# Splitting a weight slab on GpSimd and multiplying half of it over all 512 tokens, at three norms of a two-layer decoder

## The reference, cut to what matters

```
for l in range(2):
    x = layer_norm(ALPHA * x + 0.5 * swiglu(x, ffn1_w_gu[l], ffn1_w_down[l]), ...)
    x = layer_norm(ALPHA * x + hybrid_mixer(x, ...), ...)
    x = layer_norm(ALPHA * x + 0.5 * swiglu(x, ffn2_w_gu[l], ffn2_w_down[l]), ...)

def swiglu(x, w_gu, w_down):          # w_gu: 1024 x 5632, w_down: 2816 x 1024
    g, u = split(x @ w_gu, 2)
    return (silu(g) * u) @ w_down
```

## Time and profile before

| | |
|---|---|
| median of 3 runs | 2403.43 us (2401.1 to 2403.76) |
| the profiled execution: its own time | 2402.06 us |
| the profiled execution: span of the core | 2400.3 us |
| PE busy | 2386.8 us (99% of the span) |
| DVE, ACT busy | 1060.1 us (44%), 759.4 us (32%) |
| POOL busy | 16.0 us (1%) in 16 instructions |
| granted PE clock | 0.999 of full speed, mean of the execution |

### The profile page before, as it was taken

The page is one execution under the profiler, slowest core; times in us unless marked ns, Lnnn a source line. Parts: engine busy times, 40 slices in busy tenths (PEclk is TensorE's granted clock), DMA queues, the critical chain, the costliest instruction groups (busy, mean ns, idle before and its releaser), DMA issues.

```text
span 2400.3 us, 27151 instructions
## 1 busy us (share of the span) xinstructions
PE 2386.8 (99%) x11560; PEld 2005.9 (84%) x11560; DVE 1060.1 (44%) x1590; ACT 759.4 (32%) x1137; POOL 16.0 (1%) x16
## 2 busy tenths in 40 slices
PE   8999999999999999999999999999999999999998
PEld 8888888888888888888888888888888888888887
DVE  4233236554654643322543332465455647333324
ACT  4232223434442332322232221243344433232211
POOL 0000200000000000000000000000000000000000
PEclk9999999999999999999999999999999999999999
DMA  5322433223223333232232332343223323332232
GB/s 167 106 96 97 144 103 124 90 82 95 90 92 123 109 105 103 88 106 104 89 106 89 105 104 89 103 132 94 88 92 97 101 93 132 96 97 97 89 117 75
DMA packets 210536, 246.58 MB, mean 103 GB/s; under 512 B 10576, under 2 KB 172400, under 8 KB 210416
## 3 DMA queue, kind: packets, MB, share of 16 engines
q1 hardware_dynamic: 210416, 244.85, 31.4%
HBM read 238.51 MB, written 6.31 MB: 102 GB/s over the span
## 4 chain that ended last, share of the span: by engine, by line
PE 99%; DVE 1%; DMA 0%; ACT 0%; issue 0%; SPq 0%; DVEq 0%
PE main L1334 22%; PE main L1336 22%; PE main L1335 22%; PE main L1434 5%; PE main L1436 5%; PE main L1435 5%; PE side L1436 4%; PE side L1435 4%; PE side L1434 4%; PE main L1417 1%; PE main L1419 1%; PE main L1418 1%; PE side L1354 1%; PE side L1579 1%; PE main L1559 0%; PE side L1511 0%
## 5 line engine op out<-in xcount | busy, mean ns | idle before, releaser
L847 DVE TENSOR_TENSOR wl<-raw,wh 128x1024 fp32r<-128x1024 f32 (+2 forms) x437 | 494.4, 1173 | 793.0 <-ACT wh L573 792.7
L1334 PE MATMUL main<-xh,wh 128*128 128x512 f32 x2128 | 832.7, 391 | 0.3
L1336 PE MATMUL main<-xl,wh 128*128 128x512 f32 x2128 | 828.4, 389 | 0.0
L1335 PE MATMUL main<-xh,wl 128*128 128x512 f32 x2128 | 828.1, 389 | 0.0
L573 ACT ACTIVATE wh<-raw 128x1024 fp32r<-128x1024 f32 (+2 forms) x437 | 420.9, 1014 | 684.7 <-PE main L1336 300.2
L1334 PEld LDWEIGHTS main<-xh,wh 128*128 128x128 f32 x2128 | 399.5, 188 | 84.0 <-DVE mtmp L1215 1.1
L1336 PEld LDWEIGHTS main<-xl,wh 128*128 128x128 f32 x2128 | 399.5, 188 | 83.5
L1335 PEld LDWEIGHTS main<-xh,wl 128*128 128x128 f32 x2128 | 399.7, 188 | 81.6
L960 DVE SCALAR_TENSOR_TENSOR hp<-main,sil 128x512 f32<-128x512 f32 x88 | 56.7, 686 | 306.3 <-PE main L1336 297.1
L640 ACT ACTIVATE hh<-hp 128x512 fp32r<-128x512 f32 x88 | 54.1, 633 | 353.4 <-DVE hp L960 353.4
L1434 PE MATMUL main<-wh,hh 128*128 128x512 f32 x352 | 137.5, 391 | 0.0
(11 more groups left out here) (244 smaller groups left out, 2186.3 us busy)
## 6 DMA issues: line engine op xcount, KB each, us to landing
raw<-gu SPq DMA_DIRECT2D x173, 512.0 KB, 4.5
raw<-w_in SPq DMA_DIRECT2D x100, 512.0 KB, 4.6
raw<-down SPq DMA_DIRECT2D x80, 512.0 KB, 4.3
raw<-w_branch SPq DMA_DIRECT2D x24, 512.0 KB, 4.3
raw<-w_out SPq DMA_DIRECT2D x16, 512.0 KB, 4.0
raw<-w_in SPq DMA_DIRECT2D x28, 256.0 KB, 3.5
raw<-down SPq DMA_DIRECT2D x16, 256.0 KB, 3.1
spill<-xt SPq DMA_DIRECT2D x8, 512.0 KB, 6.4
```

The costliest lines, as they stand in the source:

```text
L847: ins = V.tensor_tensor(put(wl[slot]), get(raw[slot]), f32(put(wh[slot])), ALU.subtract)
L1334: T.matmul(out, hi, rh(k), start=k == 0, stop=False)
L1335: T.matmul(out, lo, rh(k), start=False, stop=False)
L1336: ins = T.matmul(out, hi, rl(k), start=False, stop=k == kk - 1)
```

## The change

- Three slabs are *pooled*: the up slab of the first pair behind a norm, at the three norms that stand ahead of a feed-forward block (norm numbers v = 2, 3 and 5; the block at the very start has no norm ahead of it). Their low part is computed by POOL and no longer by DVE. POOL waits for the same `w_hi` and counts a semaphore of its own, `w_pool`; PE's `weights_ready` and SP's loads wait for it through the new `low_at`, which for all other slabs gives `w_lo` with the pooled slabs left out of the count.
- For v > 0 `first_pair` becomes `three_parts`. Early: tokens 0 to 255 through slab g as before, and through column block m = 0 of slab g+1 only. Then the wait for all of x, and tokens 256 to 511 through slab g. Last: slab g+1, block 0 over tokens 256 to 511 and block 1 over all 512 tokens in one matmul.
- Tile 3 is transposed at k = 2 of slab g+1 and no longer at k = 4.

```diff
+        pooled = [g_ for g_ in range(2, DEPTH * S_LAYER) if g_ % S_LAYER in (1, S_FFN + S_MIX + 1)]
+
+        def low_at(g, h):
+            if g in pooled:
+                return w_pool.sem, 2 * pooled.index(g) + h + 1
+            return w_lo.sem, 2 * (g - len([p for p in pooled if p < g])) + h + 1
...
-                    sp.wait_ge(w_lo.sem, 2 * g - 2)
+                    sp.wait_ge(*low_at(g - 2, 1))
...
+            def split(g):
+                slot = g % 2
+                for h in range(2):
+                    a, b = half(g, h)
+                    pool.wait_ge(w_hi.sem, 2 * g + h + 1)
+                    G.tensor_tensor(wl[slot][:, a:b], raw[slot][:, a:b], f32(wh[slot][:, a:b]),
+                                    ALU.subtract).then_inc(*o.up(w_pool))
+
             angles()
+            for g in pooled:
+                split(g)
...
-                if L < NORMS - 1:
+                if L < NORMS - 1 and g + 2 not in pooled:
                     split(g + 2)
...
-                    pe.wait_ge(w_lo.sem, 2 * g + (2 if k else 1))
+                    pe.wait_ge(*low_at(g, 1 if k else 0))
...
+            def three_parts(v, g):
+                def products(s, k, m, tokens):
+                    W, L_ = weights(g + s)
+                    hi, lo = W[:, k, P * m:P * m + P], L_[:, k, P * m:P * m + P]
+                    out = pm[2 * s + m][:, tokens]
+                    T.matmul(out, hi, xh[:, k, tokens], start=k == 0, stop=False)
+                    T.matmul(out, lo, xh[:, k, tokens], start=False, stop=False)
+                    return T.matmul(out, hi, xl[:, k, tokens], start=False, stop=k == KD - 1)
+
+                early, late, whole = slice(0, 256), slice(256, 512), slice(0, 512)
+                pe.wait_ge(x_ready.sem, 8 * v + 4)
+                for s in range(2):
+                    if s:
+                        pe.wait_ge(acc_free.sem, v)
+                    for k in range(KD):
+                        weights_ready(g + s, k)
+                        if k == (4, 2)[s]:
+                            turn_tile(v, 2 + s)
+                        for m in range(2 - s):
+                            products(s, k, m, early)
+                pe.wait_ge(x_ready.sem, 8 * v + 8)
+                for k in range(KD):
+                    for m in range(2):
+                        ins = products(0, k, m, late)
+                ins.then_inc(slab_done.sem, 1)
+                for k in range(KD):
+                    products(1, k, 0, late)
+                    ins = products(1, k, 1, whole)
+                ins.then_inc(slab_done.sem, 1)
```

More of the change, by code:

```diff
@@ L269, in build @@
         w_lo = Signal("w_lo")
+        w_pool = Signal("w_pool")
         slab_done = Signal("slab_done")
@@ L1388, in second_rows @@
                 ins.then_inc(slab_done.sem, 1)
+            def three_parts(v, g):
[26 more added lines that the diff above has]
+                ins.then_inc(slab_done.sem, 1)
             def first_pair(v, g):
+                if v:
+                    three_parts(v, g)
+                    return
                 for part in range(2):
```

## The result

The changed kernel takes 2406.47 us (median of 20 runs, 2405.43 to 2407.95), the kernel before 2401.62 us (20 runs; 2400.89 to 2403.76): 1.0019 times as long, 95% interval 1.0013 to 1.0025, that is 4.85 us slower. The three runs of before that the prediction started from had a median 1.8 us higher than the twenty. In the profiled execution the span is 2403.8 us.

What follows compares the result with a forecast made beforehand. PE was taken as the bound, busy 2386.8 of 2400.3 us. Waits of 2.2 us less 0.9 us from joined matmuls gave +1.3 us on a median of 2403.43: 2404.7 us, range 2401.5 to 2410.5.

Steps and rivals of the forecast that it cites:

- PE is the bound: Whole kernel: PE busy 2386.8 of 2400.3 us, no wait at the norms; gain only by giving PE fewer cycles.
- Joined matmuls: Each seam: 48 matmuls of 256 tokens become 24 of 512, saving 0.31 us, 0.93 us over three seams.
- The subtractions leave DVE: Ahead of tile 3's scale: 2.34 us leave DVE, worth nothing themselves; tile 3 is ready with 0.75 us slack.
- DVE and POOL together: Tile 3's finish: POOL's reading holds DVE, so PE waits 0.74 us a seam, 2.2 us in three.
- the two bounds: PE's wait at tile 3's turn: 0.74 us by reading rate, 2.69 us if POOL holds DVE its whole instruction.
- Rival (b): Between statistics and finish of tile 3, POOL keeps DVE out for its whole instruction: +7.1 us, chance 0.18.
- what I called the same: Whole-kernel time within about 0.2%, 4.8 us, of no change; chance 0.72.
- GpSimd's own pace: POOL's halves of the slab: 2.58 us each undisturbed, ready with slack 2.7 and 2.4 us before PE asks.
- end of the early part: From tile 3's turn to the last low part of x: 2.56 us needed, PE has 2.95 us; cost nothing.
- SP's loads: SP's next load into the slab's buffer is released about when DVE released it before, at 843.33: no cost.

Runs made afterwards that it cites:

- e4: Changed kernel, but at the three seams DVE's finish of tile 3 adds two PSUM banks in place of lnb, leaving one SBUF input: 2401.35 us, 0.9999 times before.
- e6: Changed kernel, but POOL starts its second half only when DVE has finished tile 3: 2402.83 us, 1.0005 times before.
- e3: Changed kernel, but POOL multiplies the raw slab by zero in place of the subtraction, one input instead of two: 2401.10 us, 0.9998 times before.
- e5: Changed kernel, but each POOL half of 1024 columns is cut into four subtractions of 256 columns: 2403.74 us, 1.0009 times before.
- e2: Changed kernel's three parts, joined matmuls and earlier turn of tile 3, but DVE splits every slab as before: 2406.19 us, 1.0017 times before.

## Why the prediction was right, and where its sum was off

It forecast +1.3 us and +4.85 was measured: right in its bounds and in its mechanism, off by 3.55 us in its sum. That the forecast time of 2404.7 us lies only 1.8 us from 2406.47 is partly luck: it starts from a median of three runs that is 1.8 us too high, which covers half of what the sum lacks.

- **PE is the bound, and there was no wait to remove**: right. What a seam changed by is what PE lost or gained there, in every run.
- **Joined matmuls, 0.93 us**: mis-sized. e4 gives about 0.7 us. The distances used were those of unbroken rows of one kind; where the two kinds alternate, the last part of the slab takes 8.41 us and not 8.33, and these 0.08 us a seam are what is missing, within the rounding of the rows.
- **The subtractions leave DVE, slack 0.75 us at the turn of tile 3**: right that the turn needs them and gets by without a wait. e4 and e6, where the finish isn't held, show none there, though of the 0.75 us only 0.30 are left in e4 (844.22 to 844.52): the scale is held 0.33 us and starts 0.12 us later than the sum had it.
- **DVE and POOL together, a wait of 0.74 us**: this is the term that was off; it measured 1.70 us. The mechanism and its order were much as described: POOL's first half behind the finish of tile 2, the second half between scale and finish of tile 3, the same at three seams. The size of the hold was not: I priced two inputs as four times the reading of 512 columns of one, 1.60 us. e3 confirms that price for one input (0.70 us for 1024 columns), but from the end of the scale, 841.87, to the release at 843.92 two inputs took 2.05 us. That is 1.3 times 1.60, 0.45 us more, and the same length of hold delays the scale as well (0.33 us), which had no slack left. With 0.12 us by which the scale starts later behind the statistics, and 0.06 from the end of the finish to the turn, that makes the 0.96 us by which the wait exceeds 0.74. The size lies midway between the two bounds (0.74 and 2.69 us); the reason, that two inputs hold DVE nearly to the end of the instruction, is that of the upper one, whose price was too high because a half takes 2.39 us and not 2.58.
- **Rival (b), slower from a wait of 1.9 us a seam on**: the measured 1.70 us stops just short of it. With 4.85 us the kernel ended at the edge of what I called the same: the interval, 0.13% to 0.25%, lies on both sides of 0.2%. I had given this rival 0.18, though its mechanism is nearly what two inputs do.
- **The Trainium skill, SBUF — State Buffer, Who interferes with whom**: its rule of exclusion for the whole instruction came out within 0.2 us for two inputs on both sides, and e4 and e6 agree with its exemption of DVE instructions with one SBUF input. For a one-input instruction of POOL the measurement decides against "the whole instruction" (DVE released 1.93 us ahead of its end in e3). The Trainium skill's GPSIMD Engine Reference, Performance versus the Vector engine, puts the pace of a two-input instruction on GpSimd down to its two inputs taking turns at one read port; the hold of nearly the whole instruction fits that, though no run separates reading from computing inside it.
- **GpSimd's own pace, end of the early part, SP's loads**: costed at nothing, and nothing it was; e5 shows what happens once POOL is slower (8.40 us). On the early part the prediction says that 24 matmuls more hid the wait before; it was 24 in place of the 18 that are left behind the turn.

## What to carry to other kernels

Giving an engine's work to another saves only if the two don't then hold each other up: here 2.34 us taken from DVE came back as 2.27 us of DVE standing still. Before moving a two-input elementwise operation to GpSimd, list which VectorE instructions with two SBUF inputs run in that stretch and on what chain they stand; one input from PSUM (e4), or an instruction placed behind the critical one (e6), removed the clash here. And where TensorE is busy all the time, taking cover away ahead of a wait costs more than joined matmuls give back: 18 matmuls, 2.16 us, are gone from ahead of the turn, where the slack before was 0.57 us, and the joining gives 0.22 us. e2 shows the loss without any GpSimd.

## What the runs showed of the hardware

- A POOL subtraction of 1024 float32 columns takes 2.39 us alone (e6), one of 256 columns 0.73 us (e5). A slab in eight pieces took 8.40 us beside DVE, in two halves 6.56, and about half of the difference is an extra wait behind DVE.
- POOL holds a two-SBUF-input instruction of DVE until about 0.2 us ahead of its own end when it reads two inputs, and when it reads one, for 0.70 of the 2.63 us that its instruction has left once DVE's own is done (changed kernel and e3). A DVE instruction with one input from PSUM isn't held (e4: 1.28 us).
- The hold goes both ways: POOL's halves last 3.23 and 3.37 us in the changed kernel, 0.84 and 0.98 more than alone, each behind a DVE instruction that came first. A one-input multiplication on POOL is no faster than the subtraction: 2.63 us against 2.26 from the end of the DVE instruction ahead of it (e3, changed kernel).
